# Four output gate units of the delta rule, moved out of its block inverses to the input products and computed as three fp32r products

## The chip, the core and the metric

The kernel runs on one core of a Trainium2 chip. The metric is the time of one execution in microseconds (us) of device time, lower is better. Engines: TensorE multiplies (PE in the profile, PEld its weight loads), VectorE (DVE) and ScalarE (ACT) do elementwise work, GpSimd (POOL) does some of it too, SyncE (SP) starts most transfers.

## The reference

Two layers of a hybrid block over 512 latent and 256 context tokens, width 1024. Each layer projects the normalised and modulated input `h` once, and three mixers share that projection: gated DeltaNet (the delta rule), latent attention and HGRN2. An output projection and an MLP follow. Of the delta rule this matters here:

```python
zx = split_cols(hx @ w_in_l, IN_SIZES)          # q, k, v, gate (4 x 128 columns), beta, a, ...
kb = kc * bc[..., None]
lower = jnp.where(strict, jnp.einsum("nbhid,nbhjd->nbhij", kb, kc) * decay, 0.0)
t_inv = lax.linalg.triangular_solve(eye + lower, ..., lower=True, unit_diagonal=True)   # one per chunk of 64
...
y = rms_norm(o, norm_g) * jax.nn.silu(gate.astype(F32))   # the output gate, used at the very end
```

The gate is 4 units of 128 columns. It depends on `h` alone, so it can be computed at any time between the norm and the read-out.

## The kernel before

Every engine has its program written out by hand; the order in the code is the order on the engine, and semaphores join them. In each layer (`l` = 0, 1) the delta rule runs in these stages.

**Input products.** A unit is 128 output columns over all tokens: 768 in layer 0, and in layer 1, whose context outputs aren't needed, 512 for the gate, for q and for `hq` (the query of HGRN2). An fp32 product on TensorE is slow, so the units `qkv` 0 to 11 and `ba` are computed as three fp32r products: weights and activations are split in a high part (a rounded copy) and a low part (the difference), and `products` (L865 to L871) adds high*high, low*high and high*low over 8 blocks of 128 rows. ACT writes the high part of a loaded weight (`proj_high_part`), DVE subtracts it in place (`proj_low_part`), ACT empties PSUM (`padded`), DVE convolves, ACT applies SiLU. Weights come through a ring of three slots that SP fills in the order of the table `LOADS`, each load when the unit that used the slot three loads earlier is done.

**Chunk products** (L1101 to L1128): the spans, k k and k q products of six pairs of chunks (`ci` = 0 to 5), and parts of the modulation weights (`ada_point`, ending with `ada_finish`, L1028). DVE makes the first level of the inverses (L2499 to L2516) and raises `first_u`.

**Inverses** (L1161 to L1195). Five rounds of doubling, sizes 2, 4, 8, 16, 32. A round has four groups of small products on PE, `r1` for the two halves t = 0 and 1 (L1180, in the last round L1177) and `qt` for both (L1192, in the last round L1189 to L1195). DVE masks the result of `r1` (L2534) before `qt` of that half; it transposes and adds the result of `qt` (L2550, L2552, L2555) and raises `u_ready`, for which `r1` of that half of the next round waits. Between these groups stand the gate's products: `gate_work` deals out 32 steps (4 units x 8 blocks), each a plain fp32 product of `Hm` with a gate weight, 256 columns to bank 7 (L1151) and 512 to bank 6 (L1152). ACT takes each finished unit through SiLU into `gate_stage` (L2000, L2001) and sends it to DRAM (`gates_held`); it is fetched back long after.

**Meanwhile on POOL.** It clears `Xf` (L765), waits for the decays that ACT's queue broadcasts from DRAM (L1989, two transfers of 1.5 MB), multiplies them and the masks into the queries and the attention blocks (L770 to L776: 24 instructions in layer 0, 16 in layer 1), and then copies the diagonal blocks of one direction into `TT` (L781), which also needs the fourth round. ACT copies the other direction's (L2010) and the last round's results (L2015).

**Corners** (L1207 to L1221). `corner_first(0)` waits for `u_ready` of the last round, runs two dummy products (`hold_clock`, L849), and waits for `spread` = 12, which counts four copies of L2010, four of L2015 and POOL's L781, which adds four. Then follow the corner products, the transposes of v and k rows (L1138), and the scan over chunks.

Of the kernel before, what the change touches and what calls it, by code (L numbers as in the profile page):

```python
# [11 lines left out]
D, SEQ, CTX, DEPTH = 1024, 512, 256, 2  # L12
TOK = CTX + SEQ
# [25 lines left out]
for _l in range(DEPTH):  # L39
    LOADS += [(_l, "qkv", _i) for _i in range(3)] + [(_l, "ba", 0)] + [(_l, "qkv", _i) for _i in range(3, 6)]  # L40
    LOADS += [(_l, "ada", ADA_GDN_AT[_l] + _i) for _i in range(2 * ADA_GDN[_l])]
    LOADS += [(_l, "gate", _i) for _i in range(2)] + [(_l, "hq", _i) for _i in range(2)] + [(_l, "hf", _i) for _i in range(4)]
# [10 lines left out]
def landed(n):  # L53
# [4 lines left out]
UNITS = ([("norm0", 0)] + [("qkv", i) for i in range(6)] + [("ba", 0), ("qkv", 6), ("qkv", 7), ("bat", 0), ("qkv", 8), ("qkv", 9), ("gcum", 0)]  # L58
         + [("l2", i) for i in range(4)] + [("qkv", 10)] + [("l2", i) for i in range(4, 8)] + [("qkv", 11)]
         + [("gate", i) for i in range(4)] + [("hq", i) for i in range(4)] + [("grms", i) for i in range(4)]  # L60
# [41 lines left out]
def trunk_program(nc, x, ctx, c, c_ctx, w_ada, b_ada, norm_mix_pre, norm_mix_post, norm_mlp_pre, norm_mlp_post,  # L102
# [6 lines left out]
    with stack:  # L109
# [247 lines left out]
        LANDED = 16  # L357
        blocks_ready = ada_in[5]
# [145 lines left out]
        def gate_stage(u):  # L504

            return Sf[:, TOK * (u % 2):TOK * (u % 2 + 1)]
# [212 lines left out]
        def _(pool):  # L719
# [9 lines left out]
            for l in range(DEPTH):  # L729
# [34 lines left out]
                nc.gpsimd.memset(INV64.rearrange("p c h d -> p (c h d)"), 0.0).then_inc(zeros_ready, 1)  # L764
                nc.gpsimd.memset(Xf, 0.0).then_inc(zeros_ready, 1)  # L765
# [65 lines left out]
        def _(pe):  # L831
# [118 lines left out]

            def sum_squares(l, what, n0, n, mat, lo=0, part=None):
# [95 lines left out]
            for l in range(DEPTH):  # L1047
# [30 lines left out]
                last.then_inc(gemm_out, 1)  # L1078
                gemm_parts(l, "qkv", 4, [8, 9], q_high, q_low)
# [63 lines left out]
                def gate_products(u, k):  # L1143

                    if k == 0 and u:
                        pe.wait_ge(gemm_evac, number(UNITS, l, "gate", u - 1) + 1)
                    elif k == 0:
                        pe.wait_ge(ada_read, 2 * l + 1)
                    w = arrived(l, "gate", u // 2).rearrange("p (k n) -> p k n", k=KB)[:, k, 128 * (u % 2):128 * (u % 2) + 128]
                    if lo == 0:  # L1150
                        mm(ps[:, 7, CTX:2 * CTX], w, Hm[:, k, 0:CTX], start=(k == 0), stop=(k == KB - 1))  # L1151
                    last = mm(ps[:, 6, :], w, Hm[:, k, CTX:TOK], start=(k == 0), stop=(k == KB - 1))  # L1152
                    if k == KB - 1:
                        last.then_inc(gemm_out, 1)
                gate_steps = [(u, k) for u in range(4) for k in range(KB)]
                step_ends = [2, 4, 6, 8, 10] + [10 + 14 * p // 12 for p in range(1, 13)] + [27, 30, 32, 32]

                def gate_work(p):

                    for u, k in gate_steps[step_ends[p]:step_ends[p + 1]]:  # L1160
                        gate_products(u, k)  # L1161
                pe.wait_ge(p1_done, base + NC)
                for u, k in gate_steps[:step_ends[0]]:
                    gate_products(u, k)
                for g, size in enumerate(SIZES):
                    for t in range(2):
# [15 lines left out]
                        gate_work(4 * g + t)  # L1182
                    for t in range(2):
# [13 lines left out]
                        gate_work(4 * g + 2 + t)  # L1197
# [465 lines left out]
        def _(act):  # L1663
# [190 lines left out]
            for l in range(DEPTH):  # L1854
# [42 lines left out]
                def silu(u):  # L1897
# [5 lines left out]
                    af(dst[:, CTX:TOK], acc[:, CTX + 2:TOK + 2], ACT.Silu, bias=zero_col).then_inc(silu_done, 1)  # L1903
                for u in range(8):
                    padded(u)
                    if u % 2 == 1 and (l == 0 or u > 1):
                        proj_high_part(l, (2, 3, 4, 6)[u // 2])
                    if u:
                        silu(u - 1)
                    if u == 5:  # L1910
                        copied(l, "ba", 0, af(rows_held, tokens(finished(l, "ba")), ACT.Copy))
                        proj_high_part(l, 5)
# [970 lines left out]
```

## Time and profile before

| | |
|---|---|
| three runs | 2337.86, 2339.52, 2339.65 us, median 2339.52 |
| the profiled execution | 2341.05 us, its span 2339.0 us |
| PE busy | 2251.5 us, 96% of the span |
| mean granted clock of TensorE | 0.988 of full |
| gate products in the inverses, L1151 and L1152 | 192 records in the whole span (x64 and x128) |

A row of the timeline has its start, its time, its engine and line, what it writes from what it reads, the number of instructions, and in brackets how long the engine had been idle and for what. An fp32 matmul shows as two records. The granted clock (PEclk) is 1.00 at 2.4 GHz and 0.50 at 1.2 GHz.

### The profile page before, as it was taken

The numbers are of one execution on the slowest core, as the hardware profiler recorded it, in microseconds if no ns is written. First come the engines' busy times: TensorE is split into PE (matmuls) and PEld (weight loads), VectorE is DVE, ScalarE is ACT, GpSimd is POOL, SyncE is SP. The second block draws the span as 40 slices with busy tenths as digits, with TensorE's granted clock in tenths as the row PEclk, the third lists the DMA queues.
The fourth block names the chain that finished last, engine by engine and source line by source line (L and its number), as shares of the span: only waits on it lengthen the run. The fifth ranks groups of instructions, "written<-read, shape, count | busy, mean of one in ns | idle before, by whom it ended". The sixth has DMA issues, their size and how long they took to land.

```text
span 2339.0 us, 40119 instructions
## 1 busy us (share of the span) xinstructions
PE 2251.5 (96%) x17754; PEld 1833.2 (78%) x17754; DVE 1186.0 (51%) x1886; ACT 872.9 (37%) x1276; POOL 226.6 (10%) x226
## 2 busy tenths in 40 slices
PE   7999999999999999999999999999998999999998
PEld 5876698876668788888888687668885669888887
DVE  3685353287363651424333497546258556444444
ACT  5363134125463421212123546332324555232233
POOL 3013410000030100000000021511000121000000
PEclk9999999999999999999999999999998999999999
DMA  9218101134211121212121131411116301333222
GB/s 320 63 55 277 45 19 60 54 110 142 87 34 37 37 90 55 72 55 72 55 73 54 54 117 51 135 52 37 54 55 213 119 19 55 108 96 102 90 90 72
DMA packets 161684, 198.27 MB, mean 85 GB/s; under 512 B 18359, under 2 KB 129433, under 8 KB 160872
## 3 DMA queue, kind: packets, MB, share of 16 engines
q1 hardware_dynamic: 155536, 185.24, 24.3%
q10 hardware_dynamic: 5271, 10.10, 1.3%
q8 instruction: 140, 2.29, 0.4%
q0 software_dynamic: 704, 0.37, 0.2%
q14 instruction: 33, 0.26, 0.0%
HBM read 184.64 MB, written 11.06 MB: 84 GB/s over the span
## 4 chain that ended last, share of the span: by engine, by line
PE 86%; DVE 6%; ACT 4%; issue 2%; DMA 1%; POOL 0%; DVEq 0%; ACTq 0%
PE ps L1625 35%; PE ps L871 14%; PE ps L1543 5%; PE ps L1152 3%; PE ps L1021 2%; PE ps L962 2%; PE ps L1478 2%; PE ps L1582 2%; PE ps L1297 1%; PE ps L1315 1%; PE ps L858 1%; PE ps L1180 1%; PE ps L1491 1%; DVE region L2432 1%; PE ps L1192 1%
## 5 line engine op out<-in xcount | busy, mean ns | idle before, releaser
L1625 PE MATMUL ps<-region_r 128*128 128x512 f32 (+1 forms) x1536 | 376.8, 354 | 0.0
L1625 PEld LDWEIGHTS ps<-region_r 128*128 128x128 f32 x1536 | 270.3, 188 | 40.8
L1625 PE MATMUL ps<-region_r,weights_r 128*128 128x512 f32 (+1 forms) x768 | 229.6, 353 | 0.0
L2293 DVE TENSOR_TENSOR weights_r<-weights,region_r 128x2048 fp32r<-128x2048 f32 x62 | 141.9, 2289 | 119.1 <-ACT region_r L1761 119.0
L1625 PE MATMUL ps<-mixed_r,weights_r 128*128 128x512 f32 (+1 forms) x672 | 200.9, 353 | 0.0
L1625 PE MATMUL ps<-modulated_r,region_r 128*128 128x256 f32 (+1 forms) x624 | 186.7, 354 | 0.0
L1625 PE MATMUL ps<-mixed_r,region_r 128*128 128x256 f32 (+1 forms) x624 | 186.6, 353 | 0.0
L2222 ACT ACTIVATE region<-ps,cst 128x768 f32<-128x768 f32 (+1 forms) x64 | 50.4, 798 | 301.2 <-PE ps L1625 282.9
L1625 PEld LDWEIGHTS ps<-region_r,weights_r 128*128 128x128 f32 x768 | 144.3, 188 | 20.5
L2821 DVE TENSOR_TENSOR region_r<-region 128x768 fp32r<-128x768 f32 (+1 forms) x64 | 52.8, 825 | 202.2 <-ACT region L2222 202.2
L1625 PEld LDWEIGHTS ps<-mixed_r,weights_r 128*128 128x128 f32 x672 | 126.3, 188 | 18.1
L1625 PEld LDWEIGHTS ps<-modulated_r,region_r 128*128 128x128 f32 x624 | 117.2, 188 | 16.6
L1625 PEld LDWEIGHTS ps<-mixed_r,region_r 128*128 128x128 f32 x624 | 117.3, 188 | 16.5
L1761 ACT ACTIVATE region_r<-weights 128x2048 fp32r<-128x2048 f32 x62 | 118.4, 1910 | 10.6 <-DMA weights<-in_w_mlp 10.6
L871 PE MATMUL ps<-residual_r,weights_r 128*128 128x512 f32 (+1 forms) x432 | 117.4, 344 | 0.0
L2228 ACT ACTIVATE region<-ps 128x768 f32<-128x768 f32 (+1 forms) x48 | 33.9, 707 | 216.3 <-PE ps L1625 216.3
L2828 DVE TENSOR_TENSOR region<-region 128x768 f32<-128x768 f32 (+1 forms) x32 | 26.4, 826 | 138.9 <-ACT region L2228 138.9
L871 PEld LDWEIGHTS ps<-residual_r,weights_r 128*128 128x128 f32 x432 | 81.1, 188 | 10.6 <-issue 0.2
L739 POOL CAST region_r<-modulated 128x768 fp32r<-128x768 f32 (+2 forms) x24 | 26.1, 1130 | 583.8 <-ACT modulated L1830 546.7
L2300 DVE TENSOR_TENSOR weights_r<-weights,state_r 128x2048 fp32r<-128x2048 f32 x14 | 32.1, 2292 | 84.4 <-ACT state_r L1747 84.4
L1152 PE MATMUL ps<-modulated,weights 128*128 128x512 f32 x128 | 68.9, 636 | 5.2 <-issue 4.4
L871 PE MATMUL ps<-region_r,weights_r 128*128 128x256 f32 (+1 forms) x288 | 73.4, 337 | 0.0
(460 smaller groups left out, 4882.8 us busy)
## 6 DMA issues: line engine op xcount, KB each, us to landing
weights<-in_w_mlp SPq DMA_DIRECT2D x64, 1024.0 KB, 5.3
weights<-in_w_ada SPq DMA_DIRECT2D x40, 1024.0 KB, 5.3
weights<-in_w_in SPq DMA_DIRECT2D x34, 1024.0 KB, 5.3
region<-in_w_ada SPq DMA_DIRECT2D x8, 1024.0 KB, 16.6
weights<-in_w_out SPq DMA_DIRECT2D x8, 1024.0 KB, 6.6
x_kept<-residual SPq DMA_DIRECT2D x2, 3072.0 KB, 12.4
region<-decays_kept ACTq DMA_DIRECT2D x4, 1536.0 KB, 11.0
residual<-x_kept SPq DMA_DIRECT2D x2, 3072.0 KB, 9.9
```

The lines of the kernel that those rows point to most:

```text
L871: last = mm(dst[:, CTX + a:CTX + b], w[:, k, m], r[k][:, a:b], start=(k == 0 and w is high and r is r_high), stop=(k == KB - 1 and r is r_ ...
L962: last = mm(dst[:, CTX + a:CTX + b], mat, sq[:, a:b], start=(k == 0), stop=(k == n - 1))
L1021: last = mm(ps[32 * k:32 * k + 32, bank, :], cs[:, 4 * half + k, :], w[:, k, :], start=(half == 0), stop=(half == 1))
L1152: last = mm(ps[:, 6, :], w, Hm[:, k, CTX:TOK], start=(k == 0), stop=(k == KB - 1))
L1478: last = mm(dst[:, CTX + s0:CTX + s1], QH[0:96, h, 128 * qt:128 * qt + 128], KH[0:96, h, s0:s1], start=True, stop=True)
L1543: last = mm(dst[:, at:at + b - a], w[:, k, m], r[:, a:b], start=(k == 0 and part_of == "low"), stop=(k == 5 and w is low))
L1582: last = mm(o, w[:, k, m], r[:, k, a:b], start=(k == 0 and r is Hm_r), stop=(k == KB - 1 and w is low))
L1625: last = mm(dst[:, CTX + a:CTX + b], w[:, k, m], r[:, a:b], start=(k == 0 and r is r_low), stop=(k == KB - 1 and w is low))
L1761: af(mlp_high(j), ring[:, n % NSLOT, :], ACT.Copy).then_inc(w_high_ready, 1)
L2222: copied(l, what, u, af(hid[:, b, lo:], src, ACT.Relu, bias=zero_col))
L2293: v.tensor_tensor(ring_r[:, at, :], ring[:, at, :], mlp_high(j), ALU.subtract).then_inc(w_low_ready, 1)
L2821: v.tensor_tensor(hid_high[:, b, lo:], z, z, ALU.mult)
```

## The change

The gate leaves the inverses. Its four units are computed between `bat` and `qkv` 8, by `products` as three fp32r products like their neighbours; `early_gates` (PE), `early_gate_high` and `hold_gate` (ACT) and `gate_low_part` (DVE) are new, and the two gate loads move ahead in `LOADS`. The units are now staged in a block of `X`, so POOL waits for their transfers before it clears `Xf`. The small products of the inverses follow each other with nothing between them.

```diff
-    LOADS += [(_l, "qkv", _i) for _i in range(3)] + [(_l, "ba", 0)] + [(_l, "qkv", _i) for _i in range(3, 6)]
+    LOADS += [(_l, "qkv", _i) for _i in range(3)] + [(_l, "ba", 0), (_l, "qkv", 3), (_l, "gate", 0), (_l, "gate", 1), (_l, "qkv", 4), (_l, "qkv", 5)]
...
                 nc.gpsimd.memset(INV64.rearrange("p c h d -> p (c h d)"), 0.0).then_inc(zeros_ready, 1)
+                for kept_sem in gates_kept:
+                    pool.wait_ge(kept_sem, 32 * (l + 1))
                 nc.gpsimd.memset(Xf, 0.0).then_inc(zeros_ready, 1)
...
+            def early_gates(l, lo):
+
+                for u in range(4):
+                    if u % 2 == 0:
+                        pe.wait_ge(gate_low_ready, LANDED + 2 * l + u // 2 + 1)
+                    high, low = (z.rearrange("p (k n) -> p k n", k=KB) for z in (early_weights(u // 2), ring_r[:, slot(l, "gate", u // 2), :]))
+                    m = slice(128 * (u % 2), 128 * (u % 2) + 128)
+                    dst = free_pair(l, "gate", u)
+                    for k in range(KB):
+                        last = products(dst, high, low, k, m, q_high, q_low, lo)
+                    last.then_inc(gemm_out, 1)
...
+                early_gates(l, lo)
                 gemm_parts(l, "qkv", 4, [8, 9], q_high, q_low)
...
-                for u, k in gate_steps[:step_ends[0]]:
-                    gate_products(u, k)
...
                         last.then_inc(r1_out, 1)
-                        gate_work(4 * g + t)
...
                         last.then_inc(qt_out, 1)
-                        gate_work(4 * g + 2 + t)
...
+                def early_gate_high(i):
+
+                    n = LOADS.index((l, "gate", i))
+                    act.wait_ge(w_in_s[n % NSLOT], landed(n))
+                    act.wait_ge(*weights_used(LOADS.index((l, "qkv", 2 + i))))
+                    af(early_weights(i), ring[:, n % NSLOT, :], ACT.Copy).then_inc(gate_high_ready, 1)
...
                 silu(7)
+                hold_gate(0)
+                proj_high_part(l, 5)
+                for u in range(1, 4):
+                    hold_gate(u)
+                act.wait_ge(*weights_used(LOADS.index((l, "gate", 1))))
+                proj_high_part(l, 6)
                 padded(8)
...
                 for u in range(8):
-                    if u in (1, 3, 5, 6, 7) and (l == 0 or u > 1):
-                        proj_low_part(l, {1: 2, 3: 3, 5: 4, 6: 5, 7: 6}[u])
+                    if u in (1, 3, 5) and (l == 0 or u > 1):
+                        proj_low_part(l, {1: 2, 3: 3, 5: 4}[u])
+                    if u == 6:
+                        gate_low_part(0)
                     convolve(u)
+                gate_low_part(1)
+                proj_low_part(l, 5)
```

What stands on PE in layer 0 from the end of the chunk products on. L1028 is `ada_finish`, L1151 and L1152 are gate steps, L1180 an `r1` group; `modulated` is `Hm`. Before:

```order
L1028 MATMUL ps<-row_select,region 128x2 x4
L1151 MATMUL ps<-modulated,weights 128x256
L1152 MATMUL ps<-modulated,weights 128x512
L1151 MATMUL ps<-modulated,weights 128x256
L1152 MATMUL ps<-modulated,weights 128x512
L1180 MATMUL ps<-mixed,residual 64x32 x24
L1151 MATMUL ps<-modulated,weights 128x256
L1152 MATMUL ps<-modulated,weights 128x512
L1151 MATMUL ps<-modulated,weights 128x256
```

And in the changed kernel, where lines have moved:

```order
L1043 MATMUL ps<-row_select,region 128x2 x4
L1175 MATMUL ps<-mixed,residual 64x32 x48
L1186 MATMUL ps<-mixed 64x32 x48
L1175 MATMUL ps<-mixed,residual 64x32 x48
L1186 MATMUL ps<-mixed 64x32 x48
L1175 MATMUL ps<-mixed,residual 64x32 x48
L1186 MATMUL ps<-mixed 64x32 x48
```

The two gate steps ahead of the first group and those behind each group are gone; the same groups follow each other (x48 is the two halves t = 0 and 1 in a row).

What stands on ACT in layer 0 behind the SiLU of unit 6 (L1902 and L1903 before; L1895 and L1896 after). `state_r` and `region_r` are high parts of weights, `ba<-ps` is `bat`, `residual<-ps,cst` a gate unit. Before:

```order
L1747 ACTIVATE state_r_54<-weights 128x2048
L1902 ACTIVATE region<-region,cst 128x256
L1903 ACTIVATE region<-region,cst 128x512
L1913 ACTIVATE ba<-ps 128x96
L1902 ACTIVATE region<-region,cst 128x256
L1903 ACTIVATE region<-region,cst 128x512
L1894 ACTIVATE residual<-ps 128x256
L1895 ACTIVATE residual<-ps 128x512
L1706 ACT_TABLE_LOAD
```

After:

```order
L1895 ACTIVATE region<-region,cst 128x256
L1896 ACTIVATE region<-region,cst 128x512
L1902 ACTIVATE state_r_54<-weights 128x2048
L1923 ACTIVATE ba<-ps 128x96
L1895 ACTIVATE region<-region,cst 128x256
L1896 ACTIVATE region<-region,cst 128x512
L1909 ACTIVATE residual<-ps,cst 128x768
L1911 DMA gates_held<-residual 128x768
L1740 ACTIVATE region_r_52<-weights 128x2048
L1909 ACTIVATE residual<-ps,cst 128x768
L1911 DMA gates_held<-residual 128x768
L1909 ACTIVATE residual<-ps,cst 128x768
```

Between `bat` and `padded(8)` ACT now takes four gate units out of PSUM, sends them off, and writes the high parts of the last two `qkv` loads there, later than before.

## Rows read from the trace of the kernel before

**Rows 1.** Windows: stretch, its length, busy us (x instructions) by engine, clock, DMA share, GB/s.

```profile
213.74:293.31 79.57, 76.42 (x1381) 51.34 (x1380) 28.62 (x44) 14.74 (x25) 34.50 (x28) 1.00 0.30 94
1486.10:1559.54 73.44, 67.07 (x1316) 41.42 (x1316) 32.34 (x55) 14.48 (x23) 24.46 (x20) 0.93 0.28 84
107.36:124.19 16.83, 16.83 (x98) 14.54 (x96) 8.61 (x8) 4.50 (x6) 0.00 (x0) 1.00 0.20 63
124.66:141.70 17.04, 17.04 (x98) 14.70 (x96) 12.50 (x15) 10.94 (x20) 0.00 (x0) 1.00 0.19 63
1620.90:1642.60 21.70, 21.70 (x97) 17.78 (x96) 10.01 (x10) 5.74 (x6) 0.00 (x0) 1.00 0.16 49
293.31:305.00 11.69, 11.69 (x231) 10.21 (x231) 5.07 (x12) 9.01 (x20) 0.18 (x1) 1.00 0.13 49
```

**Rows 2.** Timeline of PE, layer 0, end of the chunk products to the corners.

```profile
212.69 1.05 PE L1028 MATMUL ps<-row_select,region 128*128 128x2 f32 x8 [0.72 <-ACT region L1847]
...
217.03 1.59 PE L1180 MATMUL ps<-mixed,residual 64*64 64x32 f32 x48
...
291.40 1.98 PE L849 MATMUL ps<-k_f_sb 128*128 128x512 f32 x4 [1.22 <-DVE mixed L2546]
```

**Rows 3.** Timeline of PE, layer 1, the same place.

```profile
1485.14 0.95 PE L1028 MATMUL ps<-row_select,region 128*128 128x2 f32 x8
1490.47 3.75 PE L1152 MATMUL ps<-modulated,weights 128*128 128x512 f32 x4 [4.38 <-issue]
1494.16 2.77 PE L1180 MATMUL ps<-mixed,residual 64*64 64x32 f32 x48
```

**Rows 4.** Timeline of POOL, first and last of its products, and the copy, layer 0.

```profile
227.71 1.27 POOL L770 TENSOR_TENSOR region<-region 128x512 f32<-128x512 f32 x1 [31.53 <-DMA region<-decays_kept]
...
258.48 1.46 POOL L776 TENSOR_TENSOR region<-region,k_f_sb 128x512 f32<-128x512 f32 x1
273.17 3.54 POOL L781 COPY residual<-mixed 32x768 f32<-32x768 f32 x4 [13.22 <-DVE mixed L2555]
```

**Rows 5.** Timeline of POOL, first and last of its products, layer 1.

```profile
1502.89 1.27 POOL L770 TENSOR_TENSOR region<-region 128x512 f32<-128x512 f32 x1 [21.50 <-DMA region<-decays_kept]
...
1523.51 1.27 POOL L776 TENSOR_TENSOR region<-region,k_f_sb 128x512 f32<-128x512 f32 x1
```

**Rows 6.** Timeline of DVE, steps of the inverses in layer 0.

```profile
218.74 0.96 DVE L2534 TENSOR_TENSOR mixed<-ps,masks 128x768 f32<-128x768 f32 x1 [4.56 <-PE ps L1180]
...
242.81 1.29 DVE L2555 TENSOR_TENSOR mixed<-mixed 128x384 f32<-128x384 f32 x1
...
259.59 0.58 DVE L2550 STREAM_TRANSPOSE mixed<-ps 128x384 f32<-128x384 f32 x1 [0.77 <-PE ps L1192]
260.10 0.52 DVE L2552 TENSOR_TENSOR mixed<-ps,mixed 128x384 f32<-128x384 f32 x1
260.54 0.54 DVE L2555 TENSOR_TENSOR mixed<-mixed 128x384 f32<-128x384 f32 x1
...
281.15 2.23 DVE L2541 COPY mixed<-mixed 32x768 f32<-32x768 f32 x4
286.10 1.12 DVE L2546 COPY mixed<-ps 32x384 f32<-32x384 f32 x2 [2.71 <-PE ps L1195]
```

**Rows 7.** Timeline of DVE, the last step of the chunk products in layer 1.

```profile
1489.78 0.38 DVE L2516 TENSOR_TENSOR mixed<-mixed 128x128 f32<-128x128 f32 x1
```

**Rows 8.** Timeline of ACT, layer 0: transfer of the decays, copies of the last round.

```profile
214.30 0.57 ACTq L1989 DMA_DIRECT2D region<-decays_kept  x1
...
275.95 3.44 ACT L2010 ACTIVATE residual<-mixed 32x768 f32<-32x768 f32 x4 [0.46 <-ACT state L2001]
286.10 1.97 ACT L2015 ACTIVATE residual<-ps 32x384 f32<-32x384 f32 x4 [6.70 <-PE ps L1195]
```

**Rows 9.** Windows around two falls of the clock, columns as in rows 1.

```profile
1486.00:1502.00 16.00, 11.62 (x106) 6.76 (x107) 5.40 (x15) 4.49 (x7) 0.00 (x0) 0.68 0.65 196
535.00:543.00 8.00, 5.67 (x112) 3.10 (x98) 7.97 (x22) 1.80 (x4) 0.00 (x0) 0.79 0.72 221
```

More of the change, by code:

```diff
@@ L39 @@
 for _l in range(DEPTH):
-    LOADS += [(_l, "qkv", _i) for _i in range(3)] + [(_l, "ba", 0)] + [(_l, "qkv", _i) for _i in range(3, 6)]
+    LOADS += [(_l, "qkv", _i) for _i in range(3)] + [(_l, "ba", 0), (_l, "qkv", 3), (_l, "gate", 0), (_l, "gate", 1), (_l, "qkv", 4), (_l, "qkv", 5)]
     LOADS += [(_l, "ada", ADA_GDN_AT[_l] + _i) for _i in range(2 * ADA_GDN[_l])]
-    LOADS += [(_l, "gate", _i) for _i in range(2)] + [(_l, "hq", _i) for _i in range(2)] + [(_l, "hf", _i) for _i in range(4)]
+    LOADS += [(_l, "hq", _i) for _i in range(2)] + [(_l, "hf", _i) for _i in range(4)]
     LOADS += [(_l, "hi", 0), (_l, "hgate", 0)]
@@ L55, in landed @@
     return 16 * sum(DMAS.get(what, 1) for _, what, _ in LOADS[n % NSLOT:n + 1:NSLOT])
-UNITS = ([("norm0", 0)] + [("qkv", i) for i in range(6)] + [("ba", 0), ("qkv", 6), ("qkv", 7), ("bat", 0), ("qkv", 8), ("qkv", 9), ("gcum", 0)]
+UNITS = ([("norm0", 0)] + [("qkv", i) for i in range(6)] + [("ba", 0), ("qkv", 6), ("qkv", 7), ("bat", 0)] + [("gate", i) for i in range(4)] + [("qkv", 8), ("qkv", 9), ("gcum", 0)]
          + [("l2", i) for i in range(4)] + [("qkv", 10)] + [("l2", i) for i in range(4, 8)] + [("qkv", 11)]
-         + [("gate", i) for i in range(4)] + [("hq", i) for i in range(4)] + [("grms", i) for i in range(4)]
+         + [("hq", i) for i in range(4)] + [("grms", i) for i in range(4)]
          + [("hf", i) for i in range(8)] + [("hi", i) for i in range(NC)]
@@ L1991, in _ @@
                 silu(11)
-                def hold_gate(u):
-                    if u >= 2:
-                        act.wait_ge(gates_kept[u % 2], 32 * l + 16)
-                    held = gate_stage(u)
-                    finished(l, "gate", u)
-                    if lo == 0:
-                        af(held[:, 0:CTX], ps[:, 7, CTX:2 * CTX], ACT.Silu, bias=zero_col)
-                    copied(l, "gate", u, af(held[:, CTX:TOK], ps[:, 6, :], ACT.Silu, bias=zero_col))
-                    act.wait_ge(gemm_evac, number(UNITS, l, "gate", u) + 1)
-                    act.dma_start(gates_held[l][:, u, lo:], held[:, lo:]).then_inc(gates_kept[u % 2], 16)
-                for u in range(3):
-                    hold_gate(u)
                 act.wait_ge(zeros_ready, 2 * (l + 1))
```

46 lines of the change are left out of this document (21 added, 25 removed).

## The prediction, made before the changed kernel ran

> **What bounds the kernel now.** I read the windows over the inverses first, then the timelines of PE, POOL, DVE and ACT in them, the last two windows on the clock. In the inverses of layer 0, from the end of the chunk products to the first corner product, PE is busy 76.42 of 79.57 us; in layer 1 67.07 of 73.44 at a mean clock of 0.93 [rows 1]. So PE sets the pace there, and the gate's steps are more than half of its work. POOL is in no hurry: it waits 31.53 us for the decays, does its 24 products, waits 13.22 us for the fourth round, and copies at 273.17; the corners start 16.6 us after that copy has ended [rows 1, 2, 4]. Just before them PE waited 1.22 us for DVE and then ran the two dummy products, 1.98 us [rows 2]. The question is what comes up when PE has nothing but its small groups.
>
> **The units added to the input products.** A unit in layer 0 is 24 matmuls of 256 and 24 of 512 columns. Two `qkv` units whose high weights lie in `state` took 16.83 us, two with them in `region` 17.04 us [rows 1]. The change has two of each: 33.9 us. In layer 1 the gate has 512 columns alone. The four `hq` units there, 96 such matmuls, took 21.7 us [rows 1]. Nothing else is on PE beside them, so all of it is added, 33.9 and 21.7 us.
>
> Do they run unbroken? Around them DVE is busy 8.61 of 16.83 and 12.50 of 17.04 us, ACT 4.50 and 10.94 [rows 1]. A gate load adds one ACT copy and one DVE subtraction, a unit one SiLU and one transfer. The second load's low part must be there 17 us after `bat` in layer 0 and some 10.7 us (21.4 / 2) after it in layer 1, and only the convolution of unit 7 and this subtraction stand before it. The loads of `qkv` 4 and 5 come later in the ring, but each still waits for a unit that ends 17 us or more before its own product. I take 0 for waits here; at worst a few us, which I hold in a rival. What moves the other way: `padded(8)` no longer stands behind a late SiLU, so the chain to `la_ready` is some 0.2 us better in each layer. -0.4 in all.
>
> **The inverses without the gate, as a chain.** An `r1` group started at 217.03 and DVE masked its result at 218.74, 1.71 later, in 0.96 us; a group holds PE 1.52 us (1.59 with its drain) [rows 2, 6]. A round then goes: `r1` twice (3.05), `qt` of the first half as its mask is ready by then, DVE 1.71 after its start, 1.49 us for transpose and two additions (259.59 to 261.08), and the next `r1` about 0.1 later. 3.05 + 1.71 + 1.49 + 0.1 = 6.35 us, against 6.1 of PE work. While POOL works, L2555 took 1.29 instead of 0.54 [rows 6], so a round becomes 7 to 8.5, the two halves queueing on DVE. Four rounds are 26 to 31 us. The fifth: ACT copies 3.44 and twice 1.97, DVE the masks, 2.23, and 1.12 for each half [rows 6, 8], about 8 us to `u_ready`; then the 1.98 of dummies. From 213.74 that chain would reach the corners at 250 to 253.
>
> **What is late next: POOL.** Its chain doesn't contain a gate product. The decays' second transfer was issued at 214.30 and landed at 227.71 [rows 4, 8], right after the chunk products, and nothing in the change moves that issue or the loads beside it (the first three loads behind the modulation weights are of the same size as before). From there 24 products end at 259.94, 32.2 us later; 3.54 for the copy, 263.5 at the earliest, and only then is `spread` complete. So the corners of layer 0 start at 263.5, not at 251. DVE's SBUF work now falls more densely on POOL's: five of its products took 0.2 to 0.3 more where an L2555 fell on them. With four L2555 and four copies L2541 now inside its stretch it may be 1 to 2 us later. Bounds 263.5 and 266; I take 264.5, near the row. That is 50.8 us from 213.74 where it was 79.57: 28.8 won, 33.9 paid, **layer 0 loses 5.1 us**.
>
> In layer 1 POOL has 16 products: 1502.89 to 1524.78 [rows 5], and the copy to 1528.4. The inverse chain is near that here. It can't pass its first round before DVE's last chunk step, 1490.16 [rows 7]; four rounds (two free, two beside POOL) end at 1517 to 1519, and DVE, whose copies now meet POOL, raises `u_ready` at 1524.5 to 1528, plus 2 (at half clock 4) for the dummies. Bounds 1528.4 and 1532; I take 1530.5. Before, PE came back at 1490.47, after 4.38 us, at half clock (an `r1` group took 2.77) [rows 3], which is in the 73.44. From 1486.1 the new stretch is 44.4: 29.0 won, 21.7 paid, **layer 1 gains 7.3 us**.
>
> The Trainium skill, SBUF — State Buffer, section "Who interferes with whom", bears on the meeting of DVE and POOL: the port pair that they share is an exclusive lock, held for a whole instruction, taken by a DVE copy in its fast mode or by a DVE instruction with two SBUF inputs while GpSimd reads. By that rule each of the four L2541 copies would wait for a POOL product; the L2555 of 1.29 us agrees with it. It would hurt layer 1 first, and that is rival 3.
>
> **The clock.** In layer 0 PE has nothing from about 251 to 264.5. Around the pause of 4.38 us the clock was at 0.68 over 16 us, that is 10.2 us at 1.2 GHz; around a pause of 2.3 us, 0.79 over 8 us, 3.4 us at 1.2 GHz [rows 9]. Where PE sets the pace, half of that is lost: 5.1 and 1.7 us. It does in the corners, 11.69 busy of 11.69 [rows 1]. For layer 0 I take 3.0. In layer 1 the fifth round has pauses of one to three us and then the dummies: 0 to 5.1, I take 1.5.
>
> **Sum.** Layer 0: +33.9 - 28.8 + 3.0 = +8.1. Layer 1: +21.7 - 29.0 + 1.5 = -5.8. Less 0.4: **+1.9 us**. The profiled execution took 2341.05, 1.5 above the median of 2339.52; 2339.52 + 1.9 gives 2341.4.
>
> **Rivals.**
> 1. *The clock falls inside the rounds* (slower). For: PE now has a gap in each round, in layer 1 it starts with about 2 us of pause ahead of the first group and more ahead of the second, and two pauses of 2 to 4.4 us were enough before [rows 9]. Against: in the first four rounds PE is busy 6.1 of 6.35 to 8.5. A group then takes 2.8 to 3.0 instead of 1.52. In layer 0 POOL's lateness covers it (13 us). In layer 1 the stretch at 1.2 GHz of 10.2 us costs 5.1 in the rounds, the dummies 2, and the corners of both layers pay 5.1 instead of 3.0 and 1.5. 5.1 + 2 + 2.1 + 3.6 = 12.8 over the forecast: 2354; with half of it 2348. It decides from the point at which layer 1's rounds run at 0.50. 0.25.
> 2. *The clock holds better and DVE and POOL don't disturb each other*: corners at 263.5 and 1528.4, clock 1.7 and 0. That is 1.0 + 2.1 + 1.3 + 1.5 = 5.9 less: 2335.5. 0.15.
> 3. *The lock in full*: four copies of 0.56 each wait for a POOL product of 1.27, so they take 7.3 instead of 2.2, and layer 1 starts its corners at 1532 or 1533, layer 0 at 266. +1.5 +2: 2345. 0.10.
> 4. *POOL doesn't bind at all*, because the decays land earlier than I read or the copy isn't waited for: corners at 251.5 and 1527, no pause, no loss of clock. 13 + 3.5 + 4.5 = 21 less: 2320. Nothing in the profile speaks for it. 0.04.
> 5. *The fp32r units don't run unbroken* (a low part or a PSUM pair late): a few us in each layer, 2346. 0.04. That the change doesn't do what it says I rule out by its order.
>
> **How the numbers follow.** The forecast, POOL binds and the clock falls for a few us, has 0.42, 2341.4, with its own range 2337 to 2346. The ends of all but rival 4 and the upper part of rival 1 give 2334 to 2350. A measurement of this kernel tells 0.2%, 4.7 us, from no change: faster is below 2334.8, slower above 2344.2. Faster: all of rival 4, a third of 2, a little of the forecast, 0.13. Slower: rival 1 nearly whole, 3 and 5 in good part, a seventh of the forecast, 0.37. The rest, 0.50, is within.
>
> **What would show it.** PE runs from `bat` to `qkv` 8 without a pause of over 1 us, some 34 and 22 us. The first corner product of layer 0 starts within 0.2 us of the end of POOL's copy, about 51 us after the chunk products, with PE idle for over 10 us before it, and 1.2 GHz behind. In layer 1 it starts 43 to 46 us after them. If POOL's copy ends well before the corners in layer 0, the main step is wrong; if rounds one to four take over 9 us each, rival 1 is right. If the input products grow by other than 56 us in sum, the first term is.

## The result and the profile after

| | changed | before, same chip |
|---|---|---|
| median | 2362.82 us (2360.01 to 2366.49, 5 runs) | 2339.65 us (2337.86 to 2341.84, 5 runs) |
| ratio | 1.0099, interval 1.0084 to 1.0114 | |
| span, mean clock of the profiled execution | 2360.9 us, 0.965 | 2339.0 us, 0.988 |

The change makes the kernel 23 us slower; the forecast was 2341.4, within 2334 to 2350. The input products came out as forecast, the inverses did not. First the windows: both stretches from the end of the chunk products to the first corner product, and the four gate units among the input products, in layer 0 and in layer 1 (columns as in [rows 1]).

```profile
245.61:303.10 57.49, 50.84 (x1254) 47.36 (x1253) 30.80 (x44) 10.50 (x17) 35.69 (x28) 0.51 0.21 75
1520.50:1580.77 60.27, 51.30 (x1253) 47.88 (x1253) 32.03 (x55) 11.70 (x19) 24.60 (x20) 0.52 0.17 55
123.22:156.97 33.75, 33.75 (x194) 29.47 (x193) 9.32 (x8) 9.21 (x12) 0.00 (x0) 1.00 0.30 98
1425.20:1446.85 21.65, 21.65 (x97) 17.79 (x96) 9.33 (x8) 8.53 (x12) 0.00 (x0) 1.00 0.42 133
```

The new units take 33.75 and 21.65 us without a pause (33.9 and 21.7 were forecast from [rows 1]). The stretches shrink from 79.57 to 57.49 and from 73.44 to 60.27, where 50.8 and 44.4 were forecast, and their mean clock is 0.51 and 0.52. PE's timeline in layer 0 answers to [rows 2]:

```profile
244.56 1.05 PE L1043 MATMUL ps<-row_select,region 128*128 128x2 f32 x8 [0.72 <-ACT region L1840]
245.54 4.46 PE L1175 MATMUL ps<-mixed,residual 64*64 64x32 f32 x96
249.81 5.32 PE L1186 MATMUL ps<-mixed 64*64 64x32 f32 x96
254.93 5.32 PE L1175 MATMUL ps<-mixed,residual 64*64 64x32 f32 x96
...
299.39 3.78 PE L852 MATMUL ps<-k_f_sb 128*128 128x512 f32 x4 [1.21 <-DVE mixed L2557]
303.10 0.37 PE L1200 MATMUL ps<-mixed,region 64*64 64x64 f32 x1
```

A row is now two groups, since nothing stands between them. From 249.81 each pair starts 5.12 us behind the last, 2.56 a group where [rows 2] had 1.52 to 1.59, and there is no idle time in front of any of them: PE sets the pace at half its clock. Its clock by stretches:

```profile
246.00:248.00 2.00, 2.00 (x55) 2.00 (x52) 0.49 (x2) 1.76 (x2) 0.00 (x0) 0.66 1.08 380
248.00:286.00 38.00, 37.96 (x710) 37.78 (x708) 20.66 (x29) 1.15 (x3) 26.38 (x21) 0.50 0.24 90
286.00:303.00 17.00, 10.39 (x486) 7.18 (x484) 9.33 (x14) 7.22 (x12) 9.31 (x8) 0.50 0.01 4
305.00:315.00 10.00, 10.00 (x192) 8.52 (x189) 4.63 (x11) 8.12 (x18) 0.00 (x0) 1.00 0.01 2
1525.00:1565.00 40.00, 39.95 (x818) 39.75 (x816) 21.23 (x32) 2.40 (x3) 21.18 (x16) 0.50 0.25 81
```

The clock falls between 246 and 247, about 1 us into the groups (0.66 over 246 to 248), and in the 38 us from 248 on PE is busy 37.96 of 38.00 at 0.50, that is 1.2 GHz. In the kernel before, the same place had 0.68 over 16 us in layer 1 and 1.00 throughout in layer 0 [rows 1, 9]. It is back at 1.00 only behind the two wide dummies (L852). Layer 1 does the same, with a pause of 2.21 us in front where [rows 3] had 4.38:

```profile
1519.54 0.95 PE L1043 MATMUL ps<-row_select,region 128*128 128x2 f32 x8
1522.70 4.93 PE L1175 MATMUL ps<-mixed,residual 64*64 64x32 f32 x96 [2.21 <-DVE region L2512]
```

POOL, and the last of DVE's copies before the corners of layer 0, answer to [rows 4, 6]:

```profile
258.76 1.26 POOL L773 TENSOR_TENSOR region<-region 128x512 f32<-128x512 f32 x1 [31.08 <-DMA region<-decays_kept]
...
290.16 1.46 POOL L779 TENSOR_TENSOR region<-region,k_f_sb 128x512 f32<-128x512 f32 x1
291.77 4.10 POOL L784 COPY residual<-mixed 32x768 f32<-32x768 f32 x4
```

```profile
276.59 1.56 DVE L2566 TENSOR_TENSOR mixed<-mixed 128x384 f32<-128x384 f32 x1
...
298.21 1.12 DVE L2557 COPY mixed<-ps 32x384 f32<-32x384 f32 x2 [2.85 <-PE ps L1189]
```

POOL's copy ends at 295.87, 50.3 us behind the chunk products: the chain that was to bind came out 0.5 us from the forecast (50.8). But DVE's last copy ends at 299.33 and the dummies, at half clock, take 3.78 instead of 1.98, so the corners start 7.2 us after POOL.

### The profile page after: what moved, and what is told of

Same layout as the page of the kernel before. It is cut to its first block, busy times and chain, and to the rows that moved or that the text cites. A ratio compares the mean times of both kernels' runs of the same rounds, so it can differ in the third digit from the quotient of the medians.

```text
span 2360.9 us, 40319 instructions
## 1 busy us (share of the span) xinstructions
PE 2266.5 (96%) x17850; PEld 1887.5 (80%) x17850; DVE 1196.6 (51%) x1890; ACT 879.3 (37%) x1276; POOL 227.1 (10%) x226
## 4 chain that ended last, share of the span: by engine, by line
PE 86%; DVE 7%; ACT 4%; issue 2%; DMA 1%; POOL 0%; DVEq 0%; ACTq 0%
PE ps L1618 35%; PE ps L874 18%; PE ps L1536 5%; PE ps L977 2%; PE ps L1471 2%; PE ps L1575 2%; PE ps L1036 2%; PE ps L1186 2%; PE ps L1175 2%; PE ps L1290 1%; PE ps L861 1%; PE ps L852 1%; PE ps L1484 1%; PE ps L1510 1%; PE ps L1414 1%
## 5 line engine op out<-in xcount | busy, mean ns | idle before, releaser
L1618 PE MATMUL ps<-region_r,weights_r 128*128 128x512 f32 (+1 forms) x768 | 229.6, 353 | 0.0
L2223 ACT ACTIVATE region<-ps,cst 128x768 f32<-128x768 f32 (+1 forms) x64 | 50.3, 797 | 300.9 <-PE ps L1618 283.0
L1618 PEld LDWEIGHTS ps<-region_r,weights_r 128*128 128x128 f32 x768 | 144.3, 188 | 20.6
L874 PE MATMUL ps<-region_r,weights_r 128*128 128x512 f32 (+1 forms) x384 | 102.5, 342 | 0.0
L874 PEld LDWEIGHTS ps<-region_r,weights_r 128*128 128x128 f32 x384 | 72.1, 188 | 9.0
```

The lines of the kernel that those rows point to most:

```text
L874: last = mm(dst[:, CTX + a:CTX + b], w[:, k, m], r[k][:, a:b], start=(k == 0 and w is high and r is r_high), stop=(k == KB - 1 and r is r_ ...
L1618: last = mm(dst[:, CTX + a:CTX + b], w[:, k, m], r[:, a:b], start=(k == 0 and r is r_low), stop=(k == KB - 1 and w is low))
L2223: copied(l, what, u, af(hid[:, b, lo:], src, ACT.Relu, bias=zero_col))
```

## The experiments

All have their times beside runs of the kernel before on the same chip (medians 2339.03 to 2340.21). A "group" is one of the 16 sets of 48 small products in the first four rounds, "the stretch" goes from the end of the chunk products to the first corner product.

**1. No pause ahead of the groups.**

```diff
+                pe.wait_ge(ada_read, 2 * l + 1)
+                hold_clock(ps[:, 7, :], 4)
                 pe.wait_ge(p1_done, base + NC)
```

> The changed kernel, with four dummy products of 512 columns over the whole array put ahead of the first small group of each layer's inverses, so that TensorE has hardly a pause between the chunk products and the groups; nothing is put between the groups. Theory A (the small products themselves don't keep the clock up, pause or no pause): the clock falls to 0.50 within some us of the first group and stays there, a pair of groups takes 5.12 us as in the changed kernel; the dummies add about 3.1 us in layer 0 and 1.6 in layer 1: 2367. Theory B (the pauses of 0.72 and 2.21 us ahead of the first group throw the clock down, and it then can't come back): the rounds run at 1.00, a pair takes 3.05, corners some 6.5 us (layer 0) and 12 us (layer 1) earlier: about 2346.

Measured: 2371.32 us, ratio 1.0137 (1.0120 to 1.0154). Two windows of layer 0, and PE between them:

```profile
250.00:258.00 8.00, 7.81 (x212) 6.50 (x210) 3.89 (x7) 0.00 (x0) 0.00 (x0) 0.99 0.87 325
262.00:288.00 26.00, 25.89 (x487) 25.75 (x484) 14.30 (x20) 0.00 (x0) 25.14 (x20) 0.50 0.01 3
```

```profile
257.56 0.88 PE L1177 MATMUL ps<-mixed,residual 64*64 64x32 f32 x23 [0.19 <-DVE mixed L2568]
259.60 3.50 PE L1177 MATMUL ps<-mixed,residual 64*64 64x32 f32 x73 [1.16 <-issue]
```

Neither theory as written. The dummies brought a fallen clock back, and the first round ran at full speed (3.0 us a pair), 5.8 us of small products without a pause. Then PE stood still in the middle of a group, for 1.16 us in layer 0 and 0.87 in layer 1 (the profile names no engine that it waited for); the clock fell behind that pause and stayed down, in both layers. That leaves two readings: the pause, or the small products.

**2. Small products without any pause.** The lead as above, and behind each group:

```diff
+                    for _ in range(16 if g < NS - 1 else 0):
+                        mm(ps[0:64, 7, 0:32], ones[0:64, 0:64], kf[0:64, 4, 0:32], start=True, stop=True)
```

> The changed kernel with the four wide dummies ahead of the first group (they brought the clock back to 1.00 in the run with the lead alone) and, after each of the 16 groups of rounds one to four, 16 more small dummy products (64 rows, 64 columns of weights, 32 columns moved), so that PE has no pause in a round. Theory P (small products do keep the clock, only the pauses in a round throw it down): 1.00 through four rounds, a group with its dummies 2.0 us, layer 0's corners bound by POOL, about 2350. Theory S (a stretch of small products alone loses the clock, pause or not): 0.50 some us behind the lead, a group with its dummies 3.4 us, 2390 to 2405.

Measured: 2473.47 us, ratio 1.0575 (1.0559 to 1.0591).

```profile
250.00:254.00 4.00, 4.00 (x82) 3.24 (x82) 0.96 (x1) 0.00 (x0) 0.00 (x0) 1.00 0.81 309
256.00:342.00 86.00, 86.00 (x1145) 86.00 (x1144) 20.44 (x31) 1.22 (x2) 32.11 (x26) 0.50 0.02 5
```

PE has no pause at all, 86.00 of 86.00, and the clock still falls, 4.9 us behind the start of the first group in layer 0 and 5.5 in layer 1. So this mixture of small products loses it without a pause, as theory S says. It isn't the kernel's own mixture, though: a group with its dummies takes 5.97 us where 3.4 was expected, since the 16 dummies cost over 3 us and 16 of a group's 48 products only 0.9 (why is not known), and in experiment 1 the kernel's own groups ran for 5.8 us at 1.00 and lost the clock only behind a pause. That the kernel's groups alone would lose it without any pause is therefore not shown.

**3. A wide product behind each group, without and with the lead.**

```diff
+                    if g < NS - 1:
+                        hold_clock(ps[:, 7, 0:256], 1)
```

> The changed kernel, with one dummy product of 256 columns over the whole array (about 0.5 us at 2.4 GHz) after each of the 16 small groups of rounds one to four. Theory A (wide products between the groups keep the clock up): 1.00 through four rounds, a group and its dummy 2.02 us instead of 2.56, so four rounds take 32 instead of 41; with the shorter fifth round layer 0 is then bound by POOL's copy, corners 6 to 7 us earlier, layer 1 some 11 earlier: 2346. Theory B (the clock is down whatever stands between the groups): a group and its dummy 3.56, 16 us more in each layer: 2395.

> The changed kernel with the four wide dummies ahead of the first group and one dummy of 256 columns after each of the 16 groups. Without the lead the same fill ran at 0.50 from the first group on. Theory P (a pause throws the clock down and too little wide work can't bring it back, but once it is up, no pause and some wide work keep it): 1.00 through four rounds, a group with its dummy 2.02 us, about 2350. Theory S (256 columns in 2 us are too little to keep it): 0.50 soon behind the lead, a group with its dummy 3.85, 2410.

Measured: 2407.44 us, 1.0291 (1.0276 to 1.0307) without the lead; 2366.36 us, 1.0112 (1.0097 to 1.0128) with it. The rounds of layer 0, without and with:

```profile
248.00:305.00 57.00, 57.00 (x748) 46.67 (x746) 19.86 (x31) 0.52 (x1) 30.93 (x24) 0.50 0.16 55
```

```profile
252.17:286.53 34.36, 34.36 (x801) 28.40 (x800) 21.86 (x30) 0.00 (x0) 27.60 (x21) 1.00 0.14 52
```

The same fill between the same groups runs at 0.50 when the clock was down at the first group, and at 1.00 when the lead had brought it up. It keeps the clock and doesn't bring it back. The first expectation's theory B held as to the clock, but not its reason, since the second run shows that what stands between the groups does matter; of the second, theory P held. With the fill the rounds have no pause either (34.36 busy of 34.36 us), so these two runs don't tell wide products from the lack of pauses. But a group with its dummy is 2.15 us, so with the lead (6.6 us here, part of it at 0.50) the stretch is 57.8, no shorter than the changed kernel's.

**4. The whole array, but short products**, without the lead.

```diff
+                    if g < NS - 1:
+                        hold_clock(ps[:, 7, 0:32], 8)
```

> The changed kernel, with eight dummy products of only 32 columns, but over the whole 128x128 array, after each of the 16 small groups of rounds one to four: as many columns as in the fill of 256, in products as short as the small ones. Theory A1 (what counts is how much of the array works): the clock stays at 1.00 or falls late, the fill costs about 0.25 to 0.5 us a group, 2342 to 2348. Theory A2 (what counts is that products are long, so that the array streams without a weight change): 0.50 as in the changed kernel, the fill costs 0.43 us or more a group: 2376 or more.

Measured: 2484.25 us, 1.0627 (1.0611 to 1.0644).

```profile
248.00:346.00 98.00, 98.00 (x1010) 96.00 (x1009) 21.28 (x32) 2.83 (x4) 31.28 (x25) 0.50 0.11 40
```

A fill takes 3.62 us, and the clock stays at 0.50. As experiment 3 shows, a fill without a lead can't separate A1 from A2; this stays undecided. What it does show is that short products over the whole array, 3.6 us in every 6.3, don't bring the clock back either.

**5. Half of the units moved.** Units 0 and 1 to the input products, 16 fp32 steps left in the inverses: one ahead of the first group, then three ahead in layer 0 and four in layer 1, then that for layer 0 alone.

```diff
-                for u in range(4):
+                for u in range(2):
...
-                step_ends = [2, 4, 6, 8, 10] + [10 + 14 * p // 12 for p in range(1, 13)] + [27, 30, 32, 32]
+                step_ends = [1, 2, 3, 4, 5] + [5 + 7 * p // 12 for p in range(1, 13)] + [13, 15, 16, 16]
...
+STEP_ENDS = [[3, 4, 5, 6, 7, 7, 8, 8, 9, 9, 10, 10, 11, 11, 12, 12, 13, 13, 15, 16, 16],
+             [4, 5, 6, 7, 8, 8, 9, 9, 10, 10, 11, 12, 12, 13, 13, 14, 15, 15, 16, 16, 16]]
```

> Only the first two of the four gate units move to the input products as three fp32r products; units two and three stay plain fp32 steps between the small groups, 16 steps over the 20 groups. Theory A (one step per one or two groups is enough to hold the clock): the layer 0 stretch is 79.6 less 23.8 for 16.9 more in the input products, layer 1 73.4 less 15.9 for 10.8 more: 12 us won, 2328. Theory B (half of the fill doesn't hold it, it falls between the steps): 16 groups at 2.56 instead of 1.52 and steps at twice their time, 2345 to 2370.

> Half of the units moved in both layers as in the earlier run, but with four of layer 1's 16 steps ahead of its first group (three in layer 0), and one step of 512 columns per group behind it. Theory P (only the entry was the trouble: one step of 0.99 us per group can keep the clock but not bring it back): after the pause of 4.38 us the four steps bring the clock back within 5 us and it stays, layer 1 is 5 to 7 us shorter than before instead of 27 longer: 2330. Theory S (one such step per group is too little to keep it): layer 1 falls back to 0.50 in the rounds, 2350 to 2358.

> Only in layer 0 the first two gate units move to the input products; layer 1 is as before. Of the 16 steps left in layer 0's inverses three stand ahead of the first group (one in the run with half in both layers, whose clock was at 0.50 for 10 us there and held 1.00 from then on, and whose layer 0 came out 0.8 us shorter than before). Both theories: layer 1 as before; layer 0 wins 23.8 us of fp32 steps and pays 16.9, less what the fall at the entry costs. With the fall ended after 5 to 6 us instead of 10: 2336; without a fall: 2332; if the fall lasts as long as with one step: 2338 or 2339, no difference.

Measured: one step ahead 2365.09 us, 1.0113 (1.0098 to 1.0128); three and four ahead 2342.87, 1.0012 (1.0003 to 1.0021); layer 0 alone 2342.59, 1.0012 (1.0001 to 1.0024). Layer 1's rounds, with one step ahead and with four:

```profile
1503.00:1569.00 66.00, 66.00 (x804) 47.47 (x806) 22.06 (x32) 3.55 (x5) 21.32 (x17) 0.50 0.14 53
```

```profile
1504.00:1509.00 5.00, 4.30 (x5) 1.85 (x6) 0.56 (x4) 2.48 (x4) 0.00 (x0) 0.50 0.67 204
1511.00:1546.00 35.00, 35.00 (x791) 26.47 (x790) 20.98 (x31) 0.69 (x1) 21.35 (x16) 1.00 0.17 62
```

Three more steps ahead of layer 1's first group take 22 us off the kernel (the two more in layer 0 changed nothing, 60.6 and 61.0 us): the pause of 4.38 us had thrown the clock down, four steps in a row brought it back in some 5 us, and eleven steps spread over the 16 groups then kept it, again without a pause. That is theory P, and experiment 3 once more with real work. Yet nothing is won over the kernel before. The stretch of layer 0 was 61.4 and 61.0, so 23.8 us of steps taken out gave only 18.2 and 18.6. Some 2 to 3 us are the clock at the entry, which fell there and had not in the kernel before. The rest is the fifth round: with three steps in it instead of eight (7.4 us less on PE) it went from 17.1 us only to 14.7 and 12.9, since its length isn't set by PE's work alone (more on it below). Some 4 us more went in layer 0's scans and 1.6 us at another fall of the clock at 803 us; the clock falls at other points there from run to run, and I have no cause for it.

**6. The pause filled.** The kernel before, with layer 1's first four steps (instead of two) ahead of the wait for the last chunk, and in layer 0 the 512-column half of the first step ahead of its 256-column half, which alone has to wait; the two versions with half of the units moved have that too, with more of a layer's 16 steps in the fifth round.

```diff
+                for u, k in gate_steps[:step_ends[0]]:
+                    gate_products(u, k)
                 pe.wait_ge(p1_done, base + NC)
-                for u, k in gate_steps[:step_ends[0]]:
-                    gate_products(u, k)
```

> The kernel before, without the change; only the entry to the inverses is filled: in layer 1 four gate steps (instead of two) stand ahead of the wait for the last chunk, in the pause of 4.38 us, and don't wait for the modulation columns either, since they write another bank; in layer 0 the 512-column half of a step comes first and only its other half waits. Theory A (a pause costs its own length and then some 5 us at 1.2 GHz): layer 1's stretch goes from 73.4 to about 64.5, layer 0 gains 0.5: 2330. Theory B (PE wouldn't have come back earlier since the first group hangs on DVE's last chunk step, 4.1 us in, and the clock falls for another cause): 2 to 4 us, 2336 to 2338.

> As the last, and in layer 0 the first two gate units moved to the input products; of the 16 steps left there two stand ahead of the first group, nine between the groups, five in the fifth round, which is bound by its own chain (12.7 us from its first product to the last copy, with one step or three in it) and so has room for them. Theory A (clock held): corners 58 us after the chunk products instead of 79.6, 16.9 paid: 4.5 us less than the last, 2325. Theory B (nine steps are too few to hold the clock at the entry or behind it): no better than the last, 2330 to 2345.

> Half of the gate units moved in both layers, entries filled as in the last two, layer 1 with four steps in the pause, eight between its 16 groups, four in the fifth round. Theory A: layer 1's corners 53 to 55 us after its chunk products at 10.8 paid, about 64.5 in all, as much as in the kernel with the filled entry alone or 2 us better: 2323 to 2326. Theory B (a step of 512 columns for two groups doesn't hold the clock in layer 1): 2340 or more.

Measured: 2332.76 us, 0.9964 (0.9951 to 0.9976); 2333.01, 0.9975 (0.9964 to 0.9985); 2344.98, 0.9999 (0.9977 to 1.0021). PE at layer 1's entry and the whole stretch, in the first of them:

```profile
1480.51 3.68 PE L1182 MATMUL ps<-modulated,weights 128*128 128x512 f32 x8
1484.12 1.59 PE L1214 MATMUL ps<-mixed,residual 64*64 64x32 f32 x48
```

```profile
1480.65:1546.22 65.57, 62.80 (x1316) 39.03 (x1316) 30.40 (x55) 14.45 (x23) 24.20 (x20) 1.00 0.31 94
```

The pause is gone, the clock is 1.00 over the stretch (0.93 in [rows 1]) and it takes 65.57 instead of 73.44 us, with as many instructions. This is theory A, and the version is 7 us faster than the kernel before and 30 faster than the changed one. (The profiled execution, 2327.36 us, is the fastest of its five: its span is 13.7 us below that of the trace of before, of which 7.9 are this stretch and 3 came in layer 0's scans.) Moving half of layer 0's units as well shortens that stretch by 22 us for 17 paid and shows nothing in the median: in the profiled execution layer 0 came out better, and layer 1 lost 2 us to a fall at the end of its fifth round, which its two dummies met. The version with half in both layers has two faces: of its 12 runs four took 2326.2 to 2330.2 us and eight 2344.1 to 2350.0. The profiled one is of the second kind:

```profile
1495.00:1507.00 12.00, 12.00 (x228) 8.21 (x228) 7.93 (x18) 4.48 (x7) 0.00 (x0) 1.00 0.58 158
1511.00:1551.00 40.00, 39.80 (x578) 30.39 (x582) 15.96 (x23) 2.08 (x3) 22.21 (x18) 0.50 0.03 10
```

Layer 1 starts at 1.00 and falls in the second round, behind a pause of 1.60 us in the middle of a group; a step for every two groups doesn't bring it back. That the four shorter runs are those without this fall is my reading; none of them was profiled, but their mean clock is 0.987 to 0.990 and that of the other eight 0.978 to 0.981.

**7. The change in full, the clock held.** Two wide dummies at layer 0's entry, four in layer 1's pause, all in a free bank, and a fill of 256 columns in layer 0; in layer 1 of 128, then of 256.

```diff
+                hold_clock(ps[:, 6, :], 4 if l else 2)
...
+                        hold_clock(ps[:, 6, 0:(128 if l else 256)], 1)
```

> The changed kernel with the clock held as cheaply as I can: two wide dummies at layer 0's entry, four in layer 1's pause while DVE ends the last chunk, then after each of the 16 groups a dummy of 256 columns in layer 0 (held the clock behind a lead before) and of 128 in layer 1 (not tried). Theory A (all of the miss is the clock in the rounds; the rest of the blind sum holds, POOL's copy ends some 50.5 us after the chunk products and binds in layer 0): corners 51 to 53 us after the chunk products in both layers, where the changed kernel had 57.5 and 60.3: 2362.8 less 5 and less 8, 2348 to 2351, still slower than before. Theory B (128 columns don't keep the clock in layer 1): that layer as in the changed kernel or up to 8 us longer, 2358 to 2366.

> The changed kernel with the entries filled and a dummy of 256 columns after each of the 16 groups in both layers (with 128 columns layer 1 fell to 0.50 after a pause). Theory A (256 columns hold it in layer 1 too): its fifth round starts 3.5 + 34.4 = 38 us after the chunk products, corners at 54; layer 0 as in the last run, 53. That is 4.5 and 6.3 less than the changed kernel: 2352, so the whole move would be slower than before even with the clock held. Theory B (in layer 1 it falls again within the rounds): corners at 66 or more, 2365.

Measured: 2359.18 us, 1.0105 (1.0057 to 1.0154), four runs from 2352.5 to 2385.3, with 128 columns; 2354.59 us, 1.0059 (1.0046 to 1.0073), with 256. Layer 1's rounds in the one and in the other:

```profile
1531.00:1563.00 32.00, 32.00 (x477) 29.40 (x473) 13.68 (x19) 0.00 (x0) 21.05 (x16) 0.50 0.01 2
```

```profile
1520.00:1554.00 34.00, 34.00 (x799) 28.08 (x798) 21.22 (x35) 3.02 (x5) 18.80 (x15) 1.00 0.31 96
```

With 128 columns the first six groups of layer 1 run at 1.00 without a pause for 11.6 us. Then PE waits 0.96 us for DVE, and the clock falls:

```profile
1517.00:1528.60 11.60, 11.60 (x301) 10.63 (x300) 6.91 (x15) 2.68 (x4) 0.00 (x0) 1.00 0.68 257
```

```profile
1528.19 0.49 PE L852 MATMUL ps<-k_f_sb 128*128 128x128 f32 x2
1529.63 2.77 PE L1194 MATMUL ps<-mixed 64*64 64x32 f32 x48 [0.96 <-DVE mixed L2554]
```

With 256 columns both layers have no pause and stay at 1.00 in the four rounds, and the stretches are 54.7 and 55.1. Theory A: the whole move is still 14 us slower than before. POOL's copy and the dummies of layer 0 in that run:

```profile
291.52 3.89 POOL L784 COPY residual<-mixed 32x768 f32<-32x768 f32 x4
```

```profile
295.99 3.78 PE L852 MATMUL ps<-k_f_sb 128*128 128x512 f32 x4 [1.21 <-DVE mixed L2566]
```

POOL is done at 295.41, 50.4 us behind the chunk products once more, and DVE's last copy ends only 0.5 us later; it is the dummies that are late. PE idles in the fifth round, the clock falls there, and the dummies run at 0.50, 3.78 us instead of 1.98.

## Why the prediction was wrong

How far each stage moves the later ones against the trace of before, as forecast and as found (from the starts of the same DVE instructions in both traces, the stretches from the windows):

| term | forecast | found |
|---|---|---|
| start of the kernel | 0 | -1.4 |
| input products, layer 0 and 1 | +33.9 +21.7 -0.4 | +33.3 +21.5 |
| stretch of layer 0 | -28.8 | -22.1 |
| stretch of layer 1 | -29.0 | -13.2 |
| clock behind the first corner product | +3.0 +1.5 | +0.8 +0.3 |
| scans of layer 0 | 0 | +2.3 |
| sum | +1.9 | +21.5 (spans: +21.9) |

- *The added units.* Right: priced from the rows of their neighbours, unbroken, 0.4 us off in sum.
- *POOL's chain.* Right as a time (its copy ends 50.3 to 51.3 us behind the chunk products of layer 0 in every run whose fourth round had ended by then), wrong as the bound: in no run did the corners wait for it. The nearest is layer 0 in the first run of experiment 7, where it ended 1.1 us after DVE's last copy; there the dummies, 3.53 us at half clock, ended later still.
- *The clock in the rounds.* This is the step that failed: the sum has no term for it. Against a fall I argued that "in the first four rounds PE is busy 6.1 of 6.35 to 8.5", and took busy for enough. What the runs show: PE was busy 37.96 of 38.00 us and the clock stood at 0.50 all the time, so a round took 10.24 us instead of 6.35. In layer 1 its fifth round starts 43 us behind the chunk products instead of about 32. I thought of pauses as what throws the clock down, from [rows 9], and missed what stood beside those rows: in the kernel before, the wide gate steps ran between all groups, and the clock came back among them, after 10.2 us in layer 1. Experiments 3, 5 and 7 show that with enough wide work between the groups, and the clock up at the first of them, it holds.
- *Rival 1* named the fall and gave it 0.25 and 2348 to 2354; by its own sign, rounds of over 9 us, it was the right one. Its price was too low for two reasons: it had the clock down for 10.2 us, as in [rows 9], where it was down for some 57 in each layer, with nothing wide to bring it back before the dummies; and POOL was to cover it in layer 0, where at 10.24 us a round the slack of 13 us was used up and more.
- *The fifth round.* "About 8 us to `u_ready`" was mis-sized: it took 13.1 to 13.3 us. The trace of before has the same round, at a clock of 1.00, in layer 1, from its first product on PE to the end of DVE's last copy:

```profile
1544.13 1.02 PE L1177 MATMUL ps<-mixed,region 32*32 32x32 f32 x96
```

```profile
1556.45 1.12 DVE L2546 COPY mixed<-ps 32x384 f32<-32x384 f32 x2 [2.30 <-PE ps L1195]
```

That is 13.4 us, but with eight gate steps in it and PE busy 12.28 of 13.50 us, so it doesn't tell what is left without them. The changed kernel has nothing in their place, and PE stands still between blocks of its small products:

```profile
290.74 0.25 PE L1183 MATMUL ps<-mixed 32*32 32x32 f32 x1 [1.11 <-issue]
...
294.19 0.27 PE L1183 MATMUL ps<-mixed 32*32 32x32 f32 x3 [1.91 <-issue]
...
297.92 0.26 PE L1189 MATMUL ps<-mixed 32*32 32x32 f32 x1 [2.19 <-issue]
```

I had put the round together from the durations of the copies and left these pauses out; DVE waits 2.85 us and ACT 4.07 us for PE before their last copies. PE doesn't wait there for ACT's copies of the first half, which begin here:

```profile
292.19 1.96 ACT L2018 ACTIVATE residual<-ps 32x384 f32<-32x384 f32 x4 [0.93 <-PE ps L1189]
```

The round has 480 records on PE, 192 of `r1` and 144 of each half of `qt`. By their count 15 of the second half were done when the pause of 1.91 us began, at 292.28. In experiment 3 with the lead 103 of them were done at 295.47, while ACT's copies of the first half lasted until 296.42. And behind the pause of 2.19 us a single record is left, the last of the 480, for which both engines wait. The profile names no engine for these pauses, and their cause stays open. DVE's four copies, which rival 3 had at 7.3 us, took 4.41 us in layer 0 and 3.19 in layer 1, against 2.23 before. Together with the dummies at half clock the excess is 7 us in each layer, which POOL's slack would have hidden in layer 0 had the rounds been fast.

With the clock held by the fill of experiment 7 the kernel is at 2354.6: of the 21 us missed, 8 come back with the clock, 13 don't. Its stretches are 3.9 and 10.7 us over the forecast; the fill itself is 10 us of each (16 times 0.63), and the fifth round, by subtraction, the rest, less what POOL's time would have hidden. No run shows the small groups alone at 1.00 through the four rounds, so what the forecast took for granted was never seen, and the sum without any fill stays untested.

The Trainium skill's page TensorE: Matmul & The Clock Gate (section "Why this matters for your kernels") asks for a busy TensorE and no long idle gaps between bursts of matmuls. By that rule the rounds, with hardly a gap, should have run at 2.4 GHz; the measurement disagrees: 37.96 busy of 38.00 us at 0.50 in the changed kernel, 86.00 of 86.00 in experiment 2. The same page ("What's actually happening") says that the gate follows how busy TensorE has been of late; no run here shows what it counts as busy.

What stays open: what throws the clock down within the first four rounds. Leaving out the falls at the entry, up to 2.2 us behind the start of the first group, it fell there from 1.00 six times in the profiled executions. Four of these falls (experiment 1 in both layers, the last of experiment 6 and the first of experiment 7 in layer 1) come with a pause of 0.87 to 1.60 us; only experiment 2, with its slow dummies, fell without one, in both layers. In the kernel before, a pause of 1.14 us at 252 us, between wide steps, left the clock at 1.00. No run has the kernel's own groups without pauses beyond 5.8 us, so pauses with too little wide work around them explain the record as well as the small products by themselves. Open too are: whether the length of a product or the part of the array decides; why the entry of layer 0 kept its clock in the kernel before and lost it in the profiled executions of experiments 1 to 5 with the same pauses (in those of experiment 6, where the second pause is shorter, it kept it, and in those of experiment 7 once kept and once lost it); and the few us that come and go in layer 0's scans.

## What to carry to other kernels

Work that is interleaved with small products may be what keeps TensorE's clock up; before taking it out, look at the granted clock of a stretch in which the small products run alone, and if there is none, give the half clock a price and a good chance. A pause can cost its own length and the way back. Here the way back took 3 to 6 us with four wide products in a row, 10 us with wide steps between the small groups, and did not come in 38 us of small groups alone: put independent wide work into the pause, ahead of the wait, before thinking of moving it elsewhere. A chain put together from the durations of its parts leaves out the pauses between them; set the sum against a stretch of the trace that holds the whole chain.

## What was unexpected of the hardware

- PE busy 86.00 of 86.00 us with 64x64 products of 32 columns, granted clock 0.50 throughout; it had been at 1.00 for about 5 us of the same work. In the changed kernel it was 37.96 of 38.00 us.
- The same fill, 256 columns behind each group of 48 small products, stood at 1.00 for 34.4 us or at 0.50 for 57 us, depending on the clock at its start. Four wide dummies, or four fp32 steps, brought it back in 3 to 6 us.
- Four gate steps of 512 columns placed in a pause of 4.38 us took 7.9 us off the stretch: 3.6 us less idle time of PE, and 4.3 us less busy time for the same instructions, which is the clock.
- In the last round PE stood still for 1.1 to 2.2 us between blocks of its small products, with no engine named that it waited for, once for the sake of a single record.
- With a fill of 128 columns the clock stood at 1.00 for 11.6 us without a pause, and one pause of 0.96 us was followed by 0.50 for the rest of the rounds.
